# The mixer's keys and queries turned on VectorE instead of TensorE

## The reference, cut to what matters

```python
def gla_prep(q, k, v, d_f, d_b, wd2_f, bd_f, wd2_b, bd_b):
    ...
    q = heads(q, B_DK) * (B_DK ** -0.5)
    k = heads(k, B_DK)
    ...
def gla_scan(q, k, v, log_a, s0):
    ...
    def step(s, inp):
        qc, kc, vc, gc = inp
        b = jnp.cumsum(gc, axis=2)
        b_last = b[:, :, -1:, :]
        rel = jnp.where(tri, b[:, :, :, None, :] - b[:, :, None, :, :], -jnp.inf)
        scores = jnp.einsum('bhid,bhjd,bhijd->bhij', qc, kc, jnp.exp(rel))
        o = jnp.einsum('bhij,bhje->bhie', scores, vc) + jnp.einsum('bhid,bhde->bhie', qc * jnp.exp(b), s)
        s = jnp.exp(b_last[:, :, 0, :, None]) * s + jnp.einsum('bhjd,bhje->bhde', kc * jnp.exp(b_last - b), vc)
        return s, o
```

## Time and profile before

| what | value |
|---|---|
| median of 3 runs | 2786.93 us (2786.74 to 2787.51) |
| the profiled execution | 2786.86 us, its span 2785.1 us, so 1.76 us lie around the span |
| TensorE busy (matmuls) | 2767.7 us, 99% |
| VectorE busy | 2237.9 us, 80% |
| ScalarE busy | 371.9 us, 13% |
| GpSimd busy | 373.2 us, 13% |
| granted TensorE clock | 0.999 of full speed |

### The profile page before, as it was taken

How to read it: one execution, slowest core, us unless ns; L and a number is a source line. 1 busy time by engine, 2 the same in 40 slices (tenths; PEclk the granted TensorE clock), 3 DMA queues, 4 the chain that set the end, 5 groups by cost and what they waited for, 6 DMA issues and landing times.

```text
span 2785.1 us, 35903 instructions
## 1 busy us (share of the span) xinstructions
PE 2767.7 (99%) x13604; PEld 2426.1 (87%) x13604; DVE 2237.9 (80%) x3565; ACT 371.9 (13%) x701; POOL 373.2 (13%) x462
## 2 busy tenths in 40 slices
PE   9999999999999999999999999999999999999998
PEld 8888888888888888888888888888888888888887
DVE  7988787989999999998886568978888888766554
ACT  3221112001111111110002121211200000000000
POOL 1112231011112121120111002201011111000000
PEclk9999999999999999999999999999999999999999
DMA  8787666677766666667786455557566776565553
GB/s 272 240 256 225 207 205 204 212 242 229 215 206 207 211 214 210 209 220 271 267 262 182 146 159 144 154 164 227 173 215 213 220 220 205 174 175 190 174 174 122
DMA packets 276381, 571.81 MB, mean 205 GB/s; under 512 B 25370, under 2 KB 26778, under 8 KB 275696
## 3 DMA queue, kind: packets, MB, share of 16 engines
q1 hardware_dynamic: 244528, 460.18, 53.7%
q0 software_dynamic: 31248, 109.01, 12.4%
q10 hardware_dynamic: 432, 0.34, 0.0%
HBM read 565.49 MB, written 3.93 MB: 204 GB/s over the span
## 4 chain that ended last, share of the span: by engine, by line
PE 79%; issue 16%; DVE 3%; DVEq 1%; POOLq 0%; POOL 0%; DMA 0%; ACT 0%; ACTq 0%
PE PS L560 73%; DVEq L1091 1%; PE PS L641 1%; PE PS L603 1%; PE PS L729 0%; PE PS L704 0%; PE PS L570 0%; DVE sums L1092 0%; DMA ring<-in_w_in 0%; DVEq L1109 0%; DVE ring L1083 0%; DVE x_tok L1691 0%; PE PS L719 0%; PE PS L993 0%; PE PS L894 0%
## 5 line engine op out<-in xcount | busy, mean ns | idle before, releaser
L560 PE MATMUL PS<-sums,mem 128*128 128x256 f32 x4056 | 1206.3, 379 | 0.0
L560 PE MATMUL PS<-ring,mem 128*128 128x256 f32 x3788 | 1071.1, 379 | 0.0
L560 PEld LDWEIGHTS PS<-sums,mem 128*128 128x128 f32 x4056 | 770.6, 190 | 104.8
L560 PE MATMUL PS<-ring,act_t 128*128 128x256 f32 x3076 | 832.8, 379 | 0.1
L560 PEld LDWEIGHTS PS<-ring,mem 128*128 128x128 f32 x3788 | 715.5, 190 | 97.7 <-issue 1.6
L560 PEld LDWEIGHTS PS<-ring,act_t 128*128 128x128 f32 x3076 | 578.6, 190 | 77.5 <-issue 1.6
L1082 DVE TENSOR_TENSOR sums<-ring 128x512 f32<-128x512 f32 x431 | 313.0, 726 | 278.9 <-PE PS L560 253.2
L1203 DVE SCALAR_TENSOR_TENSOR mem<-mem,small 128x512 f32<-128x512 f32 x480 | 358.5, 768 | 34.0 <-DMA mem<-in_w_mod 2.9
L1092 DVE TENSOR_TENSOR sums<-sums,ring 128x512 f32<-128x512 f32 x431 | 311.1, 722 | 34.3 <-issue 2.1
L1094 DVE TENSOR_TENSOR sums<-sums,ring 128x512 f32<-128x512 f32 x431 | 302.9, 703 | 32.7 <-issue 0.9
L560 PE MATMUL PS<-sums,act_t 128*128 128x256 f32 x1092 | 324.8, 379 | 0.0
(11 more groups left out here) (273 smaller groups left out, 1253.6 us busy)
## 6 DMA issues: line engine op xcount, KB each, us to landing
ring<-in_w_in SPq DMA_DIRECT2D x240, 512.0 KB, 3.8
mem<-in_w_mod POOLq DMA_DIRECT2D x192, 512.0 KB, 5.0
ring<-in_w_up SPq DMA_DIRECT2D x176, 512.0 KB, 3.8
ring<-in_w_ffn_in SPq DMA_DIRECT2D x176, 512.0 KB, 3.7
ring<-in_w_down SPq DMA_DIRECT2D x88, 512.0 KB, 4.6
ring<-in_w_ffn_out SPq DMA_DIRECT2D x88, 512.0 KB, 3.8
ring<-in_w_out SPq DMA_DIRECT2D x64, 512.0 KB, 4.5
ring<-in_w_branch_a SPq DMA_DIRECT2D x16, 512.0 KB, 3.8
```

The costliest lines, as they stand in the source:

```text
L560: mm = pe.matmul(product(g, j), of(j, 2 * (c if part is None else part) + q), weights(j, n, q), start=lead and j in OPENS, stop=tail, skip ...
```

## The change

TensorE no longer turns keys or queries. VectorE does it in 32 instructions, 16 for each, of 32 partitions by 256 elements. They go in quarters of the tokens: a quarter is four instructions, one for each quarter of the features. ScalarE no longer copies the turned keys and queries out of PSUM; it scales the queries in place in `q_tok`, 128 partitions by 1024 elements, before they are turned. The quarters stand in the table at (1, 2): two of the keys; (1, 3), behind the gather: one of the keys; (2, 0): the last of the keys and two of the queries; (2, 1): the last two of the queries. The waits for the turned queries move: out of TensorE's items and VectorE's `level_close`, into GpSimd's `qe`. `rem` now waits for the cumulated decays, and `cum` for the log decays, which before stood with the turns.

```diff
-                      (1, 0): [("la", 1)], (1, 1): [("la_end", 1)], (1, 2): [("kt",)],
-                      (1, 3): [("gather", 1), ("cum",)], (2, 0): [("qt",)], (2, 1): [("rem", 0), ("rem", 1)],
+                      (1, 0): [("la", 1)], (1, 1): [("la_end", 1)], (1, 2): [("kt", 0), ("kt", 1)],
+                      (1, 3): [("gather", 1), ("cum",), ("kt", 2)], (2, 0): [("kt", 3), ("qt", 0), ("qt", 1)],
+                      (2, 1): [("qt", 2), ("qt", 3), ("rem", 0), ("rem", 1)],
...
@@ TensorE
-                    elif item[0] == "kt":
-                        kept_all(pe, G0["mix"] + K_GROUP)
+                    elif item[0] == "cum":
                         pe.wait_ge(s["la_ready"], 2)
-                        for hd in range(GH):
-                            for h in range(2):
-                                mm = pe.transpose(PS[:, 4 + hd // 2, (hd % 2) * T + h * P:(hd % 2) * T + (h + 1) * P],
-                                                  k_tok[:, h, hd * P:(hd + 1) * P], ident[:])
-                        mm.then_inc(s["kt_done"], 1)
-                    elif item[0] == "cum":
-                        pe.wait_ge(s["kt_kept"], 1)
...
-                    elif item[0] == "qt":
-                        kept_all(pe, G0["mix"] + Q_GROUP)
-                        pe.wait_ge(s["cum_kept"], 1)
-                        for hd in range(GH):
-                            for h in range(2):
-                                mm = pe.transpose(...)
-                        mm.then_inc(s["q_turned"], 1)
                     elif item[0] == "rem":
                         r = item[1]
+                        pe.wait_ge(s["cum_kept"], 1)
...
@@ VectorE
+            def heads_turn(src, dst, a, done):
+                for b in range(4):
+                    rows = slice(32 * b, 32 * b + 32)
+                    from_ = src[32 * a:32 * a + 32].rearrange("p h (f c) -> p h f c", f=4)[:, :, :, rows]
+                    to = dst[rows].rearrange("p f (h t) -> p h f t", h=2)
+                    op = ve.transpose(to[:, :, :, 32 * a:32 * a + 32], from_)
+                if a == 3:
+                    op.then_inc(s[done], 1)
+                    ve.drain()
...
+                    elif item[0] == "kt":
+                        if item[1] == 0:
+                            ve.drain()
+                        heads_turn(k_tok, k_t, item[1], "kt_kept")
+                    elif item[0] == "qt":
+                        if item[1] == 0:
+                            ve.wait_ge(s["q_scaled"], 1)
+                        heads_turn(q_tok, q_t, item[1], "q_kept")
...
@@ ScalarE
-                    elif item[0] == "kt":
-                        act.wait_ge(s["kt_done"], 1)
-                        act.copy(k_t.rearrange("p (a b) t -> p a (b t)", a=2), pair(4)).then_inc(s["kt_kept"], 1)
...
-                    elif item[0] == "qt":
-                        act.wait_ge(s["q_turned"], 1)
-                        act.activation(q_t.rearrange("p (a b) t -> p a (b t)", a=2), pair(4), ACT.Copy,
-                                       scale=float(HD) ** -0.5).then_inc(s["q_kept"], 1)
+                    elif item == ("qt", 0):
+                        kept_all(act, G0["mix"] + Q_GROUP)
+                        act.activation(q_tok[:], q_tok[:], ACT.Copy, scale=float(HD) ** -0.5).then_inc(s["q_scaled"], 1)
...
@@ GpSimd, item "qe"
+                        pool.wait_ge(s["q_kept"], 1)
```

More of the change, by code:

```diff
@@ L314, in build @@
             "forms_ffn2", "forms_h", "forms_h2", "forms_hx", "forms_m", "forms_mix", "forms_w2", "hidden_turned", "x_first", "w_first", "sums_first", "gates_squashed",
-            "g_opened", "gate_loaded", "gate_ready", "gate_stored", "hidden_done", "job_acc", "kdec_ready", "kt_done", "kt_kept", "la_done", "la_exp", "la_ready",
+            "g_opened", "gate_loaded", "gate_ready", "gate_stored", "hidden_done", "job_acc", "kdec_ready", "kt_kept", "la_done", "la_exp", "la_ready",
             "levels_loaded", "lv_diff", "lv_done", "lv_exp_k", "lv_exp_q", "lv_k", "lv_q", "lv_taken", "masks_loaded", "max_ready",
             "merged", "mixer_loaded", "mod_ready", "o_done", "o_rs", "o_sq", "o_sum", "out_stored", "post_added", "post_dotted", "var_ready", "z_squared",
-            "post_rs", "post_scaled", "post_squared", "probs_ready", "probs_t_ready", "probs_turned", "q_kept", "q_turned",
+            "post_rs", "post_scaled", "post_squared", "probs_ready", "probs_t_ready", "probs_turned", "q_kept", "q_scaled",
             "proj_turnable", "qe_exp", "qe_ready", "rem_done", "rem_exp", "rpb_loaded", "rstd_ready", "scores_done",
@@ L923, in _ @@
                         mm.then_inc(s["cum_done"], 1)
-                    elif item[0] == "qt":
-                        kept_all(pe, G0["mix"] + Q_GROUP)
-                        pe.wait_ge(s["cum_kept"], 1)
-                        for hd in range(GH):
-                            for h in range(2):
-                                mm = pe.transpose(PS[:, 4 + hd // 2, (hd % 2) * T + h * P:(hd % 2) * T + (h + 1) * P],
-                                                  q_tok[:, h, hd * P:(hd + 1) * P], ident[:])
-                        mm.then_inc(s["q_turned"], 1)
                     elif item[0] == "rem":
                         r = item[1]
+                        pe.wait_ge(s["cum_kept"], 1)
                         mm = pe.matmul(PS[:, 6 + r, :], tri[:, 2 + r, :], la[:, r, r, :], start=True, stop=True)
@@ L936, in _ @@
                     elif item[0] == "wst":
-                        pe.wait_ge(s["q_kept"], 1)
                         pe.wait_ge(s["mixer_loaded"], 16)
@@ L967, in _ @@
                             pe.wait_ge(s["lv_taken"], lv)
-                        else:
-                            pe.wait_ge(s["q_kept"], 1)
                         size, across = {0: (HP, 1), 1: (HP // 2, 1)}.get(item[2], (HP // 2, 0))
@@ L1547, in level_close @@
                     ve.wait_ge(s["rem_done"], 3)
-                    ve.wait_ge(s["q_kept"], 1)
                 if l < 7:
```

## The result

The changed kernel takes 2791.01 us (median of 20 runs, 2789.8 to 2792.0), the kernel before 2787.0 us on the same chip. One of the 20 runs of the kernel before took 5980.1 us; the median isn't touched by it. The ratio is 1.0014, with an interval of 1.0008 to 1.0020. That is under the 0.2% by which the prediction counts a change as none, but the interval leaves out 1: the kernel is slower, by a little. The time lies inside the forecast range of 2786.3 to 2791.3, 0.3 us from its end. The forecast was a loss of 2.5 us; 4.0 were measured. So the direction was right, and 1.5 us have to be found. The profiled run took 2790.9 us with a span of 2789.1 (before 2786.86 and 2785.1).

A forecast was written before the change was run, and what follows sets the result against it. TensorE bounds the kernel and sheds 1.74 us, but VectorE's 14.84 us of added work exceeds 11.98 us of holes; 2.89 us late less 0.36 leaves 2.5: 2786.86 + 2.5 = 2789.4 us, range 2786.3 to 2791.3.

The forecast's parts named there:

- What decides: Gather of group 2, third operation, needed by Q7 of chunk (3, 0): no margin, so VectorE's 2.5 us lateness passes on.
- The turns and the holes: VectorE before level (0, 0): 32 turns at 0.449 us plus drains, 14.84 us, against 11.98 us of holes; 2.89 us late.
- L1535 beside GpSimd: Level (0, 0)'s multiplication, formerly L1553, meeting GpSimd: 1.65 us instead of 2.01, giving back 0.36 us.
- The clock: Rival: TensorE's clock halves for one chunk after the four waits, adding 6.0 us to 2795.4 us; chance 0.04.
- The sum: From VectorE's stretch to the gather of group 2: 2.89 us late less 0.36 given back, a 2.5 us loss.
- The waits on TensorE: Levels (0, 0) and (0, 1), then Q2 and Q7 of (3, 0): 1.2, 0.7, 1.5, 0.5 us; 3.9 together.
- What was costed at nothing: Moved waits of `cum`, `rem` and `qe`, DMA issues, steps' sums and SyncE's loads: no time lost.
- The queries' gather: VectorE's gather that chunk (2, 0) needs: delayed by the turns but hidden, by 0.9 us.
- The scaling: ScalarE scaling the queries before their turns: 1.02 us, bounds nothing to 1.87 us, hidden by over 3 us.
- VectorE has room: Rival: turns fit VectorE's holes before level (0, 0), so the full 1.74 us is won, 2785.1 us; chance 0.07.
- A part is won back: Rival: GpSimd meets VectorE less, or ScalarE's exponentials come sooner; 2788.5 or 2787.6 us; chance 0.18 for 2786 to 2788.4.
- The range: Whole kernel: 2786.3 to 2791.3 us, leaving out the full gain, the clock and a tail of dearer turns.

The follow-up runs named there:

- change again: The changed kernel run once more unaltered, on one chip with the second filled run: 2791.96 us against 2787.47 for the kernel before, ratio 1.0015.
- waits filled: Changed kernel, with TensorE multiplying ones in its waits before levels (0, 0), (0, 1) and chunk (3, 0): 2790.79 us, then 2791.81 us in the second run.
- eight turns added: Against keys early: last quarter of the queries turned twice more at (2, 1), with three drains, 40 turns in all; 2789.95 us, ratio 1.0009 to the kernel before.
- decays late: Changed kernel with the two products of keys by decays moved from (2, 2) to (3, 0), behind the gather of group 2: 2789.30 us against 2787.33 before.
- keys only: Against the kernel before: only the keys turned on VectorE (16 turns), queries still on TensorE and ScalarE; 2786.72 us against 2787.30, ratio 0.9998.
- queries only: Against the kernel before: only the queries turned on VectorE and scaled on ScalarE, keys still on TensorE; 2786.38 us, ratio 0.9997.
- keys early: Changed kernel with the keys' four quarters moved to (1, 0) and (1, 1), ahead of the log decays: 2785.94 us, ratio 0.9995 to the kernel before.
- keys early, gap moved: Against keys early: 70 idle VectorE drains added in its wait at (0, 2), shifting later instructions in its stream; 2786.10 us, ratio 0.9995 to the kernel before.
- keys early, decays late: Changed kernel with keys turned at (1, 0) and (1, 1), and products of keys by decays behind the gather of group 2: 2785.69 us, ratio 0.9994.

## Why the prediction came out as it did

All the D that were measured, in us. "Clock" is what is left of D when the gather's lateness is taken off, where a stretch behind it shows a clock under 1.00. The last column is the distance from L835 to the end of the span, less that of the kernel before, in the same profiled run (spans are known to 0.1 us).

| kernel | median less before's | D | gather late | clock | to the span's end |
|---|---|---|---|---|---|
| change | +4.0 | +4.35 | +3.17 | 1.18 | +4.3 |
| change again | +4.5 | +4.76 | +3.17 | 1.59 | +4.9 |
| waits filled, twice | +3.5, +4.3 | +3.12, +3.12 | +3.18, +3.18 | 0 | +3.1, +5.1 |
| eight turns added | +2.6 | +2.77 | +1.76 | 1.01 | +3.5 |
| decays late | +2.0 | +1.90 | +1.96 | 0 | +2.1 |
| keys only, queries only | -0.6, -0.9 | -0.89, -0.88 | -0.89, -0.89 | 0 | -0.9, -0.9 |
| keys early | -1.4 | -1.47 | -1.40 | 0 | -1.5 |
| keys early, gap moved | -1.2 | -1.75 | -1.75 | 0 | -0.8 |
| keys early, decays late | -1.6 | -1.75 | -2.46 | 0 | -1.5 |

Where the clock stayed at 1.00, D is the lateness of the gather to within 0.1 us, down to a floor of -1.75. The 1.18 us of the change can be read from its stretches too: 0.13, 0.50 and 0.22 of 2.00 us each make 1.70 us of TensorE's speed lost. Half of the 0.26 us of waiting at Q7 isn't a loss, and 0.31 us would have been a wait there anyway (0.57 us in the filled kernel, 0.26 here), which leaves about 1.26. In the repeat nothing is taken off, for the clock fell as that wait ended, and 1.59 were measured. Point by point:

- *What decides.* Right: the gather of group 2, reached through a stretch of VectorE that had no hole. The decays' move and the keys' earlier place show it from both sides.
- *The turns and the holes.* The price was right: 0.448 us a turn in the rows of eight. The lateness at L1535 of level (0, 0) came out at 3.18 us instead of 2.89 (1654.88 - 1652.04, and 0.34 because this run started the stretch sooner). I had let a turn behind a plain operation start 0.61 us after it, as another plain one does (1625.73 to 1626.34 in the kernel before); it starts after 0.72 or 0.73 (1634.83 to 1635.55), at three places: 0.35 us.
- *L1535 beside GpSimd.* 1.65 us, exactly the value taken from the earlier trace rows, and 0.36 given back.
- *The gap.* Not in the sum: 0.44 us ahead of L1075 at 1664.73, where a step's operation normally follows with 0.10. That is 0.34 us more.
- *The clock.* The sum put it at nothing, and it was a rival with a chance of 0.04 and 6.0 us. The clock did fall after the waits that I had listed, but it was low for only 3.4 us (by the stretches, 1.70 us lost at half speed) and took 1.2 us, not 6.0. Its argument against, from the kernel's start, was a poor row: there the waits were others. This is the largest part of what the sum lacked.
- *The sum.* 2.5 + 0.35 + 0.34 = 3.19 for the gather, against 3.17 measured; with the clock's 1.18, 4.37 against D = 4.35. The waits on TensorE were forecast as 1.2, 0.7, 1.5 and 0.5 us and are 1.76, 1.23, 2.07 and 0.26, of which 0.17 and 0.33 us stand at the two levels in the kernel before as well. The order and the places are right. The last is short because the clock had already fallen, so that TensorE came to Q7 later: at full clock, in both filled kernels and in the repeat, it is 0.57.
- *What was costed at nothing.* Right. The queries' gather didn't hold (2, 0). The scaling takes what I took:
```profile
1636.13 1.06 ACT L2136 ACTIVATE mem<-mem 128x1024 f32<-128x1024 f32 x1
```
It ends 4.9 us before the queries' first turn, the fifth of the twelve that begin at 1640.21, which starts at 1642.10. From `wsum` on the two profiled runs are equal to 0.01 us.
- *The rivals.* "VectorE has room" is false for both halves together where the change puts them, and true for each of them alone, which I hadn't considered. "A part is won back" didn't happen.
- *The range.* That it held is partly luck. Its upper end, 4.4 us over the kernel before, was set to leave the clock out, and the clock came; it took little enough to fit. The repeat, at 4.5 us over, would have missed it.

What is open: why the medians of the filled kernels lie 0.4 and 1.2 us above their D (that with the gap moved 0.5 us), and what sets the landing of the weights at 1714.9 us. The last column of the table shows how far D reaches: where it is over D by more than 0.5 us, level (0, 6) accounts for most of it in that profiled run (1.96 us over its usual 0.33 in the second filled run, 0.71 with the gap moved, 0.75 with eight turns added). That a low clock costs 1.0 to 1.6 us of this stretch is shown by the traces; that it costs this much of the kernel's time isn't.

## What to carry to other kernels

Work that goes to a second engine is free only up to the holes ahead of the next place where the first one needs it: add up the holes, not the busy share (16 turns each won 0.88 us, 32 lost 4.35). When the holes don't do, put the work ahead of an earlier hole, or move later what the next wait doesn't need; the first turned the loss into a gain in the trace (4.35 lost to 1.47 won), the second cut it to 1.90. And a sum of waits on TensorE is not the bill yet: look at the granted clock behind them, and then whether the next transfer lets the time through.

## What the hardware showed that I had not expected

- TensorE's granted clock fell to 0.50 after three waits of 1.76, 1.23 and 2.07 us within some 12 us, in the repeat only at the end of a fourth of 0.57, and with eight turns added during the third of waits of 0.70, 1.23 and 1.72; not after 1.75, 0.33, 1.77 and 0.57. Filling the waits with products kept it at 1.00, twice. Three falls and one run without don't show a rule.
- VectorE has gaps of 0.42 to 0.45 us without a releaser at fixed places of its instruction stream, in the change at 1601.50 and again at 1664.73, 86 operations or, with drains and waits on semaphores, 128 instructions of the trace later. Seventy drains put ahead moved it to other work, and with a path that has no margin it cost 0.28 us. Not every such place shows a gap: none does in the keys only run and in that with eight turns added.
- VectorE starts a stream transpose 0.72 us after a tensor-tensor of 0.69 us, where another tensor-tensor that waits for nothing starts after 0.61.
